# Operand placement in SBUF: the mixer's output and FFN 2's operands, 64 or 128 bytes off the weights modulo 512

## The reference

```python
h = h + 0.5 * ml[:, 2] * swiglu(modulate(rmsnorm(h, g0), ml[:, 0], ml[:, 1]), ffn_w_in[0], ffn_w_out[0])
hc = ...                                    # the same FFN 1 on the context
pl = modulate(rmsnorm(h, g1), ml[:, 3], ml[:, 4]) @ w_in     # 2048 -> 5152, also on hc
y = concat(pool_mixer(pl), gated_delta_net(pl, states of the context's scans))
h = h + ml[:, 5] * (y @ w_out)
h = h + 0.5 * ml[:, 8] * swiglu(modulate(rmsnorm(h, g2), ml[:, 6], ml[:, 7]), ffn_w_in[1], ffn_w_out[1])
return rmsnorm(h, final_g)

def swiglu(u, w_in, w_out):                 # w_in 2048 x 11264, w_out 5632 x 2048
    gate, up = split(u @ w_in)
    return (silu(gate) * up) @ w_out
```

## Time and profile before

| | us |
|---|---|
| median of 3 runs | 2868.89 (2867.87 to 2872.45) |
| the profiled execution | 2869.56 |
| its span, first to last instruction | 2867.7 |
| mean granted TensorE clock | 0.993 |
| PE, VectorE, ScalarE, GpSimd busy | 2813.9, 1609.8, 986.9, 219.4 |
| HBM read | 560 MB, 210 GB/s with the writes |

### The profile page before, as it was taken

The page is one execution under the profiler, slowest core; times in us unless marked ns, Lnnn a source line. Parts: engine busy times, 40 slices in busy tenths (PEclk is TensorE's granted clock), DMA queues, the critical chain, the costliest instruction groups (busy, mean ns, idle before and its releaser), DMA issues. The chain is left out here.

```text
span 2867.7 us, 42535 instructions
## 1 busy us (share of the span) xinstructions
PE 2813.9 (98%) x15728; PEld 2379.9 (83%) x15728; DVE 1609.8 (56%) x2068; ACT 986.9 (34%) x1443; POOL 219.4 (8%) x373
## 2 busy tenths in 40 slices
PE   6999999999999999999999999999999999999998
PEld 4688888888888888888888888878988888888887
DVE  5567667677676652223226666655675555555444
ACT  3222222222222222111214555544355444444443
POOL 0000000000000000000101003555120000000001
PEclk9999999999999999999999999999999999999999
DMA  9866676667888855555553666685556666666664
GB/s 372 304 209 217 197 224 217 202 219 244 316 304 302 311 193 197 194 184 174 191 193 101 170 184 190 200 262 170 161 166 195 190 190 190 190 190 191 191 191 146
DMA packets 410337, 604.63 MB, mean 211 GB/s; under 512 B 52961, under 2 KB 303841, under 8 KB 401521
## 3 DMA queue, kind: packets, MB, share of 16 engines
q1 hardware_dynamic: 361824, 419.52, 47.1%
q10 hardware_dynamic: 48400, 183.63, 18.6%
HBM read 560.02 MB, written 43.02 MB: 210 GB/s over the span
## 5 line engine op out<-in xcount | busy, mean ns | idle before, releaser
L1988 DVE TENSOR_TENSOR wl<-raw,wh 128x1024 fp32r<-128x1024 f32 x638 | 784.2, 1230 | 918.4 <-ACT wh L1510 917.2
L1510 ACT CAST wh<-raw 128x1024 fp32r<-128x1024 f32 x638 | 667.7, 1047 | 1462.6 <-PE ps L785 1054.1
L784 PE MATMUL ps<-xl,wh 128*128 128x512 f32 (+1 forms) x2560 | 968.5, 378 | 0.0
L783 PE MATMUL ps<-xh,wh 128*128 128x512 f32 (+1 forms) x1904 | 722.7, 380 | 0.8 <-DVE wl L1988 0.7
L785 PE MATMUL ps<-xh,wl 128*128 128x512 f32 (+1 forms) x1904 | 716.5, 376 | 0.0
L784 PEld LDWEIGHTS ps<-xl,wh 128*128 128x128 f32 x2560 | 482.0, 188 | 89.5
L783 PEld LDWEIGHTS ps<-xh,wh 128*128 128x128 f32 x1904 | 358.8, 188 | 75.6 <-issue 8.9
L785 PEld LDWEIGHTS ps<-xh,wl 128*128 128x128 f32 x1904 | 358.5, 188 | 66.4
L2170 DVE SCALAR_TENSOR_TENSOR acc<-abuf,cT,acc 128x1024 f32<-128x1024 f32 x300 | 371.2, 1278 | 23.3 <-DMA abuf<-in_w_ada 22.9
L791 PE MATMUL ps<-x,wh 128*128 128x512 f32 x1408 | 349.6, 393 | 2.6 <-DVE x L2058 2.6
L791 PEld LDWEIGHTS ps<-x,wh 128*128 128x128 f32 x1408 | 254.6, 189 | 48.5 <-issue 2.8
(11 more groups left out here) (298 smaller groups left out, 2429.5 us busy)
## 6 DMA issues: line engine op xcount, KB each, us to landing
raw<-in_ffn_w_in SPq DMA_DIRECT2D x704, 256.0 KB, 3.3
raw<-in_ffn_w_out SPq DMA_DIRECT2D x176, 512.0 KB, 3.6
abuf<-in_w_ada ACTq DMA_DIRECT2D x64, 1024.0 KB, 6.9
abuf<-in_w_ada ACTq DMA_DIRECT2D x96, 512.0 KB, 4.0
xl<-d_h ACTq DMA_DIRECT2D x80, 512.0 KB, 3.2
ada_t<-in_ada SPq DMA_DIRECT2D x64, 512.0 KB, 9.5
raw<-in_w_in SPq DMA_DIRECT2D x128, 256.0 KB, 3.4
raw<-in_w_out SPq DMA_DIRECT2D x32, 512.0 KB, 4.2
```

The source lines that it names most:

```text
L783: mm(out, ah, bh, start=first, stop=False, skip_group_check=reopened)
L784: mm(out, ah, bl, start=False, stop=False, skip_group_check=reopened)
L1510: nc.scalar.copy(wh[:, t % HL, :], raw[:, t % RAW, :]).then_inc(hi_done, 1)
L1988: tt(tl, raw[:, t % RAW, :], th.bitcast(F32), ALU.subtract).then_inc(lo_done, 1)
```

## The change

Seven edits of the allocation, all of them sizes and one moved tile. `apart2` grows by 64 bytes; `gate_c` (128 bytes) goes behind `adac`, and `apart6` (64 bytes) takes its place, so that `wh` and `wl` keep their addresses; `apart3`, `apart4` and `apart1` shrink by 64, 64 and 128 bytes. `ha`, `hb`, `hc`, `x2`, `yh`, `yl` and with them `raw`, `h_lat` and `scale_c` then start 128 bytes past the weights modulo 512. `sg`, `hf`, `nacc`, `h_ctx` and the mixer's tiles move by 128 bytes. `xh`, `xl`, `hth`, `htl`, `acc` and `abuf` stay. The instructions are the same.

```diff
@@ -246,7 +246,7 @@
             xh = sb("xh", [P, KT, NTOK], F32R, stack=both)
             xl = sb("xl", [P, KT, NTOK], F32R, stack=both)
             b1 = sb("b1", [P, KT], stack=both)
-        sb("apart2", [P, KT])
+        sb("apart2", [P, 2 * KT])
         with ExitStack() as hid_a:
             ha = sb("ha", [P, HID_A, 2, SEQ], F32R, stack=hid_a)
         yh = sb("yh", [P, KT, SEQ], F32R)
@@ -262,13 +262,14 @@
         h_lat = sb("h_lat", [P, KT, SEQ])
         raw = sb("raw", [P, RAW, TILE])
         scale_c = sb("scale_c", [P, 5, KT])
-        gate_c = sb("gate_c", [P, 2, KT])
+        sb("apart6", [P, KT])
         wh = sb("wh", [P, HL, TILE], F32R)
         wl = sb("wl", [P, HL, TILE], F32R)
         cols = sb("cols", [P, N_COLS])
         cT = sb("cT", [P, 2 * KT])
         gate8 = sb("gate8", [P, KT])
         adac = sb("adac", [P, 2, MOD_COLS])
+        gate_c = sb("gate_c", [P, 2, KT])
         n_ms = sb("n_ms", [P, 4])
         n_rstd = sb("n_rstd", [P, 4])
         ident = cols[:, C_IDENT:C_IDENT + P]
@@ -280,7 +281,7 @@
 
         with ExitStack() as st:
             with ExitStack() as hid_b:
-                sb("apart3", [P, 112], stack=hid_b)
+                sb("apart3", [P, 96], stack=hid_b)
                 hb = sb("hb", [P, HID_B, 2, SEQ], F32R, stack=hid_b)
             h_ctx = sb("h_ctx", [P, KT, SEQ], stack=st)
             sg = sb("sg", [P, 2, NTOK], stack=st)
@@ -291,13 +292,13 @@
 
             rsum = nacc
             with ExitStack() as hid_c:
-                sb("apart4", [P, 112], stack=hid_c)
+                sb("apart4", [P, 96], stack=hid_c)
                 hc = sb("hc", [P, K_FF - HID_A - HID_B, 2, SEQ], F32R, stack=hid_c)
             cpad = sb("cpad", [P, KT, 32], stack=st)
             arow = sb("arow", [P, 2, ADA_W], stack=st)
             with ExitStack() as first:
                 ada_t = sb("ada_t", [P, ADA_RING, KT // ADA_Q, ADA_W], stack=first)
-            sb("apart1", [P, 6 * KT], stack=st)
+            sb("apart1", [P, 4 * KT], stack=st)
             hth = sb("hth", [P, GROUP_FF, NTOK], F32R, stack=st)
             htl = sb("htl", [P, GROUP_FF, NTOK], F32R, stack=st)
             with ExitStack() as closing:
```

## The result

The changed kernel takes 2883.31 us (2881.44 to 2886.85, five runs) against 2868.89 us, a ratio of 1.0051 with a 95% interval of 1.0040 to 1.0062. It is slower by 14.4 us, outside the predicted range of 2857 to 2878. The profiled execution has a span of 2881.4 us, 13.7 more than before. The lines of the changed file are one further down: the wide "high" matmul of FFN 2 is line 792, the narrow "low" one line 796.

A forecast was written before the change was run, and what follows sets the result against it. The prediction took TensorE's start-to-start matmul distance in FFN 2 as the bound. Faster low matmuls (-5.0 us) and output projection (-1.3 us), with highs unchanged, took 2868.9 to 2862.6 us; range 2857 to 2878.

The forecast's parts named there:

- What bounds the kernel: FFN 2's up and down projections: time is the number of matmuls by their start-to-start distance, 344.7 ns a pair.
- part (3): Scratch and mixer tiles moved by 64 or 128 bytes: 0 us, covered by VectorE and ScalarE slack; scan 1 us either way.
- Parts (1): Weights and FFN 1's operands stay in place, so FFN 1 and the head projection's matmuls change by 0 us.
- Part (2): Operands of FFN 2 and the output projection go from 64 to 128 bytes past the weights: -6.3 us.
- one more step of the same 2 to 4 ns brings all of them to the floor: FFN 2's low matmuls all reach 113.4 ns, from 115.8 on average: 5.0 us saved.
- the highs as they are: FFN 2's wide matmuls stay at 228.9 ns: 0 us, within bounds of 226.7 to 231 ns.
- rival B: Larger distance also frees FFN 2's highs, to 226.7 ns as at distance 0: -10.9 us, 2858.0; chance 0.17.
- The two kinds of lows: FFN 2's low matmuls at 113.4 and 118.1 ns, taken as a sign that weight load and stream meet in SBUF.
- E: Weight load meets the stream in every narrow matmul, FFN 2's lows at 120 ns: +9.6 us, 2878.5; chance 0.20.
- D: Only distance modulo 128 counts, so 128 is as 0 in FFN 2 and output projection: +5.0 us, 2873.9; chance 0.12.
- C: Distance doesn't matter beyond not being 0, load and stream passing once anyway or independent: 0 us, 2868.9; chance 0.18.
- The rule against it: Skill page: TensorE never waits and weight loads have their own read port, so addresses can't matter: 0 us.

The follow-up runs named there:

- experiment 1: The changed kernel with only the streamed operands put back at 64 bytes from the weights, all other moves kept; 2870.11 us, ratio 1.0003.
- d0: The kernel before with the operands of the output projection and FFN 2 at distance 0 from the weights; 2882.11 us, ratio 1.0039.
- h64l192: The kernel before with FFN 2's low weights alone 128 bytes further on, operands at 64 from wh and 192 from wl; 2868.27 us, ratio 0.9996.
- d192: The kernel before with the operands of the output projection and FFN 2 at 192 bytes from the weights; 2872.16 us, ratio 1.0014.
- d448: The kernel before with the operands of the output projection and FFN 2 at 448 bytes, scratch tile osq also moved; 2872.66 us, ratio 1.0014.

## Why the prediction was wrong

**What bounds the kernel: right.** FFN 2 is TensorE's start-to-start distance by the number of pairs; 33 x 0.414 us is as much as the whole difference. VectorE, ScalarE and DMA kept their slack, as the cover in part (3) said.

**Parts (1) and (3): right.** FFN 1 is unchanged to the last digit, and experiment 1 prices all other moved tiles at nothing, within 0.14%.

**Part (2), the sum: wrong, in its choice and in the upper bound of the highs.** The step that failed is "one more step of the same 2 to 4 ns brings all of them to the floor" for the lows, and "the highs as they are". The lows went to 118.6, not 113.4: +6.0 us in place of -5.0, inside their bounds but at the other end. The highs went to 232.6, past the 231 set as the upper bound: +7.6 us in place of 0. The output projection lost 0.3 us in place of gaining 1.3. The choice for the lows and the bound of the highs came from a straight line through two places, 0 and 64. The table shows that there is no line: at 32 and 96, on both sides of 64, highs cost 4 ns more. Nor were the rows at 0 good prices for FFN 2. At 0 a wide matmul reaches the 226.7 of the earlier trace rows only behind five others (`d0`: 229.8 on average), so rival B's state was not to be had at any of the nine distances tried in a stage that changes kind every eight.

**The two kinds of lows: seen, but read wrongly.** I took the slow kind as the price of a meeting that a larger distance would take away. `h64l192` shows both kinds at one distance; which one comes is a matter of how the run is entered. At 128 there is no fast kind at all.

**The rivals.** E was the nearest: slower, lows in the slow kind (118.6, E said 120), deciding where the lows' mean passes 115.8. It had the highs "unchanged or a little worse" and priced them at nothing, and the highs were the larger half, so that 2878.5 was still 5 us short; the range, cut just below it, had no room for both terms going the wrong way. D came out wrong in its repeat (`d0` is not 128), but its held a true hint that I used only in its favour: distances 256 bytes apart took the same time, which fits a repeat of 128 and one of 256 alike, and of these `d0` against the change rules out 128, while `d192` against `d448` fits 256. C is out: the distance does matter. It also had the load wrong: a block of weights is 512 bytes, not several times 512, against 2048 bytes of a wide stream.

**The rule against it.** The Trainium skill, page "SBUF — State Buffer", says in section "SBUF: two separate sides" that TensorE never waits for anyone there, and the table in section "A bandwidth-pool intuition that's wrong (but worth ruling out)" gives weight loads an independent port. By this the result would have been no change. The runs differ: moving 28 blocks of one operand by 64 bytes made their wide matmuls 3.6 ns longer, and moving the weights by 128 bytes cost 1.3% of the kernel. Whatever the ports are, the two reads are not independent in time.

**Left open.** Why 256 bytes, why -64 is good for narrow and bad for wide matmuls, and what holds the two rhythms, is not shown by these runs. The repeat itself rests on two pairs of places, and the one of 128 and 384 was seen only in different stages. That the load and the stream disturb each other is shown by their distance and by the eighth high in `h64l192`; the structure of the memory behind it is not.

## What to carry to other kernels

Where TensorE streams without a gap and loads new weights for every matmul, the place of the streamed operand relative to the weights was worth up to 2.5% of the stage here, 8.6 ns of a pair of 512 and 256 columns. It shows in start-to-start distances and hardly in the busy time of one matmul (396 ns in place of 393 for a high). It can't be extrapolated: try it in steps of 32 bytes over 256, in the stage itself with its own mix of widths, and hold every other tile in place. Here a stage of wide matmuls alone ran better with operands and weights at the same place than 384 bytes apart, the only other place tried for it; the mix did best at 64 bytes.

## What the runs showed of the hardware

The effect of the distance repeats every 256 bytes in both pairs seen (192 as 448, 128 as 384). A wide float32r matmul takes 226.7 ns start to start when undisturbed at the 2.4 GHz level, and 232 to 234 on average at every distance tried but 0 and 64 (229.0 at 64). The load underneath a matmul, for the next one, is what disturbs it: with only the low weights moved, the high with a low load underneath took 236 ns in place of 229. Narrow matmuls have two lasting rhythms, 113.4 and 117.7 ns, at one and the same distance, chosen by the matmul before them (at distance 64: fast behind a high of 231 or 232 ns, slow behind one of 225 to 230), and wide ones at distance 0 need about five matmuls after a disturbance to come back to 226.7. Scratch tiles of the other engines had no effect that could be seen in the places tried.
